# Expert rows added into residual rows in DRAM by an indirect accumulating transfer, tiles loaded back, and the beginning by chunks

## The chip, the cores and the metric

One NeuronCore of a Trainium2 chip runs the whole program. The metric is the device time in microseconds of one execution, the median over several. Engines by their short names in the profile: PE is TensorE, DVE is VectorE, ACT is ScalarE, POOL is GpSimd, SP is SyncE, which here only issues DMAs.

## The reference

A trunk of two layers over 1024 tokens of width 1024, all in float32. Each layer has a mixer (attention in layer 0, a causal convolution module in layer 1) and then a mixture of experts; each is normed and modulated by a conditioning vector and added to x through a gate. Cut to what matters:

```python
for layer in range(DEPTH):                                  # DEPTH = 2
    mod = silu(c) @ w_ada[layer] + b_ada[layer]
    sh1, sc1, g1, sh2, sc2, g2 = split(mod, 6)
    h = rms_norm(x, norm1_g[layer]) * (1 + sc1) + sh1
    y = attention(h) if layer == 0 else conv_module(h)
    x = x + g1 * y
    h = rms_norm(x, norm2_g[layer]) * (1 + sc2) + sh2
    # 16 experts in 4 groups; best group, top 2 in it, weights w normed to sum 1
    for t, (e, w) in routed(h):                             # 2 experts for each token
        moe[t] += w * ((silu(h[t] @ w_gate[e]) * (h[t] @ w_up[e])) @ w_down[e])
    x = x + g2 * moe
return rms_norm(x, final_g)
```

## The kernel before

**Stages.** The program goes through: the modulation's first pieces and the first norm (to 44 us), the projections of attention (to 386), attention (to 740), routing and experts of layer 0 (to 1165), the end of that layer and the convolution module (to 1612), routing and experts of layer 1 (to 2033), the end. x lies in SBUF as eight tiles of 128 tokens (`xtile(t)`), except during attention and where it is read again.

**Units.** The 2048 pairs of token and expert are sorted by expert and cut into units of 32 rows, about 73 in each layer; how many an expert has is known only at run time (`bounds`). A unit's 32 rows are spread as quarters over the 128 partitions, so a row of 1024 is four rows of 256. The token of each slot is in `slot_tok`, made by matmuls of one-hot matrices (L1621). For a unit, GpSimd copies its column of `slot_tok` (L585) and gathers its 128 quarter rows from `h_dram` by an indirect DMA (`gather`, L573), VectorE turns, scales and moves them (L1210, L1212, L1216), TensorE multiplies by gate and up (`gate_up`, L1633), ScalarE takes the silu (L768), VectorE multiplies (L1220) and turns (L1224), TensorE multiplies by down (`down`, L1643), and VectorE multiplies by the gate g2 into one of two buffers `yo` (`keep_y`, L1228). ScalarE's queue then stores the unit's rows with four plain DMAs to `y_dram` (L773). The engines run these in written order, in loops over two units each; TensorE has the order gate_up(b), down(b-1).

**Weights.** SyncE loads 6 MB for each expert into one of three sets as soon as the set is free (L370, L374).

**End of a layer.** When all rows are stored (`rows_stored`), GpSimd gathers for each tile two rows of `y_dram` for each token (L596, 16 DMAs of 512 KB), VectorE adds them, weighted, to x (`combine`, L1276 and L1278), then ScalarE squares for the next norm (L646, L652), VectorE scales (L979), TensorE transposes (L1438), and ScalarE and VectorE keep the halves (`norm_keep`, L659 and L985). After layer 1 the next norm is the final one: L972 writes each row tile to one of two buffers, and SyncE stores it (L462).

**The beginning.** Tiles 0 to 3 are normed and transposed while four pieces of w_ada load, and are kept only once the modulation is made (L1005), since keeping scales and shifts.

Of the kernel before, what the change touches and what calls it, by code (L numbers as in the profile page):

```python
# [37 lines left out]
TABLE = MAXBLK + 4  # L38
PARTS = 4
# [20 lines left out]
def trunk(nc, x, c_col, b_ada, final_g, vec_cols, b_out, b_router, w_router, w_ada, w_qkv, w_o, w_in, w_out,  # L60
# [6 lines left out]
    h_dram = [nc.dram_tensor(f"h_rows{l}", (T, D), f32, kind="Internal").ap() for l in range(2)]  # L67
    y_dram = [nc.dram_tensor(f"expert_rows{l}", (MAXBLK * UNIT, D), f32, kind="Internal").ap() for l in range(2)]

    ctx = ExitStack()  # L70
    with ctx:
# [24 lines left out]
        tokid, tile_first = sb("tokid", [P, TT]), sb("tile_first", [P, TT])  # L96
# [6 lines left out]
        idx_now = sb("idx_now", [P, 2], i32)  # L103
        quarter_of = sb("quarter_of", [P, 1])
# [11 lines left out]
        def hrow(n, t):  # L116
# [48 lines left out]
        ygat = [kv[:, 2 * D * b:2 * D * (b + 1)].rearrange("p (k d) -> p k d", k=2) for b in range(4)]  # L165
        hots = hflat[:, 2304:2304 + TT * (3 * UNIT + TABLE)].bitcast(mybir.dt.bfloat16)
        low_hot, low_row, low_tile = (
            hots[:, 2 * TT * UNIT * k:2 * TT * UNIT * (k + 1)].rearrange("p (n s) -> p n s", s=UNIT) for k in range(3))
        high_hot = hots[:, 6 * TT * UNIT:6 * TT * UNIT + 2 * TT * TABLE].rearrange("p (n b) -> p n b", b=TABLE)
# [16 lines left out]
        ada_loaded = [sem(f"ada_loaded{u}") for u in range(2)]  # L186
        bias_loaded = [sem(f"bias_loaded{u}") for u in range(2)]
# [40 lines left out]
        stored = both("stored")  # L228
        y_gathered = [[sem(f"y_gathered{l}{b}") for b in range(4)] for l in range(2)]
        x_added, rows_stored = both("x_added"), both("rows_stored")  # L230
        y_stored = [[sem(f"y_stored{l}{u}") for u in range(2)] for l in range(2)]
# [97 lines left out]
        def _(sp):  # L329
# [12 lines left out]
            for n in range(FIRST_ADA):  # L342
                sp.dma_start(ada_first[n], w_ada[n]).then_inc(ada_loaded[0] if n == 3 else at_loaded[(n + 2) % 3], 16)
            for j in range(8):
# [17 lines left out]
            for l in range(2):  # L362
                sp.wait_ge(stored[l], 16)
# [45 lines left out]
            for k in range(2):  # L409
                first_expert(0, 0, k)  # L410
# [22 lines left out]
            for j in range(10):  # L433
# [5 lines left out]
                if j == 8:  # L439
                    load_shifted(4)  # L440
# [1441 lines left out]
```

## Time and profile before

| | us |
|---|---|
| runs (3) | 2074.67, 2076.95, 2079.11; median 2076.95 |
| the profiled execution | 2082.66, of which the span 2080.9 |
| PE busy | 1910.5 (92%) |
| DVE, ACT, POOL busy | 1182.0, 487.0, 303.6 |
| mean granted clock | 0.953 |

A row of a timeline gives the start in us, the duration, the engine and line, what it writes and reads, and in brackets how long its engine was idle before and what released it. In the chain of waits, each row is a start, a duration and the work that the end waited for. The DMA share is the mean busy share of the core's 16 DMA engines. Queue q1 is SyncE's, q10 ScalarE's, q0 GpSimd's.

### The profile page before, as it was taken

The numbers are of one execution on the slowest core, as the hardware profiler recorded it, in microseconds if no ns is written. First come the engines' busy times: TensorE is split into PE (matmuls) and PEld (weight loads), VectorE is DVE, ScalarE is ACT, GpSimd is POOL, SyncE is SP. The second block draws the span as 40 slices with busy tenths as digits, with TensorE's granted clock in tenths as the row PEclk, the third lists the DMA queues.
The fourth block names the chain that finished last, engine by engine and source line by source line (L and its number), as shares of the span: only waits on it lengthen the run. The fifth ranks groups of instructions, "written<-read, shape, count | busy, mean of one in ns | idle before, by whom it ended". The sixth has DMA issues, their size and how long they took to land.

```text
span 2080.9 us, 49950 instructions
## 1 busy us (share of the span) xinstructions
PE 1910.5 (92%) x19736; PEld 1184.4 (57%) x19736; DVE 1182.0 (57%) x2105; ACT 487.0 (23%) x1029; POOL 303.6 (15%) x464
## 2 busy tenths in 40 slices
PE   5999999999999968999999589999899699999990
PEld 2444444445666646777777357655444467777770
DVE  3547600378889953333333569999995433333336
ACT  3101000456777730000000230010535000000002
POOL 0001030000000012222222400000001122222223
PEclk8999999899999979999999789999999799999995
DMA  9556620100430098777985803033106899854446
GB/s 393 219 202 258 228 62 0 41 11 11 185 150 1 11 367 301 264 280 289 348 329 210 306 9 107 1 119 109 51 0 240 303 408 407 321 208 172 172 172 257
DMA packets 122491, 391.43 MB, mean 188 GB/s; under 512 B 23808, under 2 KB 44928, under 8 KB 118272
## 3 DMA queue, kind: packets, MB, share of 16 engines
q1 hardware_dynamic: 72432, 303.48, 38.5%
q0 software_dynamic: 21904, 66.99, 9.0%
q10 hardware_dynamic: 28032, 19.17, 3.1%
q8 instruction: 95, 1.56, 0.3%
q14 instruction: 28, 0.23, 0.0%
HBM read 337.33 MB, written 47.49 MB: 185 GB/s over the span
## 4 chain that ended last, share of the span: by engine, by line
PE 84%; DVE 8%; DMA 4%; ACT 1%; issue 1%; SPq 0%; POOL 0%; ACTq 0%; DVEq 0%; POOLq 0%
PE ps L1633 24%; PE ps L1643 12%; PE ps L1685 10%; PE ps L1459 9%; PE ps L1570 5%; PE ps L1514 5%; PE ps L1528 4%; PE ps L1541 4%; PE ps L1553 4%; DVE kv L1343 3%; PE ps L1757 3%; DMA kv<-in_w_ada 2%; PE ps L1722 1%; PE ps L1438 1%; DVE pbuf L1027 1%
## 5 line engine op out<-in xcount | busy, mean ns | idle before, releaser
L1633 PE MATMUL ps<-kv,hT 128*32 128x256 f32 x5504 | 388.4, 380 | 2.1 <-DMA kv<-in_w_gate_up 2.1
L1633 PEld LDWEIGHTS ps<-kv,hT 128*32 128x32 f32 x5504 | 241.3, 110 | 65.4 <-issue 4.3
L1343 DVE SCALAR_TENSOR_TENSOR kv<-kv,cols 128x640 f32<-128x640 f32 (+1 forms) x330 | 266.2, 807 | 11.2
L1685 PE MATMUL ps<-hT,ring 128*128 128x320 f32 (+1 forms) x768 | 225.7, 455 | 6.3 <-ACT hT L659 6.3
L1216 DVE TENSOR_TENSOR hT<-hT,modc 128x256 f32<-128x256 f32 x146 | 62.1, 425 | 296.9 <-PE ps L1633 296.9
L1459 PE MATMUL ps<-hT,ring 128*128 128x512 f32 x512 | 223.8, 598 | 1.6 <-ACT hT L659 1.6
L768 ACT ACTIVATE hT<-ps 128x128 f32<-128x128 f32 x146 | 40.6, 278 | 747.4 <-PE ps L1633 747.4
L1040 DVE TENSOR_TENSOR_SCAN pbuf<-hT 128x128 f32<-128x128 f32 (+7 forms) x128 | 173.3, 1354 | 46.2 <-ACT hT L710 45.8
L1685 PEld LDWEIGHTS ps<-hT,ring 128*128 128x128 f32 x768 | 146.4, 192 | 82.2 <-ACT hT L659 7.0
L1459 PEld LDWEIGHTS ps<-hT,ring 128*128 128x128 f32 x512 | 97.4, 192 | 126.1 <-issue 123.3
L1633 PE MATMUL ps<-ring,hT 128*32 128x256 f32 x2560 | 151.5, 389 | 15.9 <-DVE hT L1216 14.2
L573 POOL DMA_INDIRECT hT<-h_rows,idx_now x150 | 146.2, 974 | 112.6 <-POOL idx_now L585 109.9
L1228 DVE TENSOR_TENSOR hT<-ps,bcC 128x256 f32<-128x256 f32 x146 | 62.0, 425 | 160.4 <-PE ps L1643 159.3
L1633 PE MATMUL ps<-hT 128*32 128x256 f32 x1280 | 146.0, 379 | 0.0
L1633 PEld LDWEIGHTS ps<-ring,hT 128*32 128x32 f32 x2560 | 101.5, 113 | 57.7 <-issue 19.3
L1643 PE MATMUL ps<-kv,hT 128*32 128x256 f32 x2112 | 127.8, 379 | 1.5 <-DVE hT L1224 1.5
L585 POOL COPY idx_now<-slot_tok 128x1 int32 x146 | 48.2, 330 | 455.8 <-DVE hT L1210 455.8
L1633 PEld LDWEIGHTS ps<-hT 128*32 128x32 f32 x1280 | 92.0, 110 | 37.6 <-issue 0.2
L1757 PE MATMUL ps<-ring,hT 128*128 128x512 f32 x256 | 112.4, 593 | 0.0
L1514 PE MATMUL ps<-ring,hT 128*128 128x512 f32 x256 | 110.0, 592 | 0.0
L1027 DVE SCALAR_TENSOR_TENSOR pbuf<-kv,cond,pbuf 128x512 f32<-128x512 f32 x140 | 105.3, 752 | 5.0
L710 ACT ACTIVATE hT<-ps 128x128 f32<-128x128 f32 (+7 forms) x128 | 84.5, 660 | 94.2 <-PE ps L1531 88.4
(251 smaller groups left out, 2395.8 us busy)
## 6 DMA issues: line engine op xcount, KB each, us to landing
kv<-in_w_gate_up SPq DMA_DIRECT2D x136, 512.0 KB
kv<-in_w_ada SPq DMA_DIRECT2D x21, 2048.0 KB, 7.8
ring<-in_w_gate_up SPq DMA_DIRECT2D x80, 512.0 KB
kv<-in_w_down SPq DMA_DIRECT2D x48, 512.0 KB
ring<-in_w_down SPq DMA_DIRECT2D x40, 512.0 KB
hT<-in_w_gate_up SPq DMA_DIRECT2D x40, 512.0 KB
expert_rows<-hT ACTq DMA_DIRECT2D x584, 32.0 KB
ring<-in_w_in SPq DMA_DIRECT2D x32, 512.0 KB, 11.9
```

The costliest lines, as they stand in the source:

```text
L573: pool.indirect_dma_start(out=xg[u], out_offset=None, in_=h_dram[l].rearrange("t (q d) -> (t q) d", q=QUARTERS), in_offset=bass.IndirectOf ...
L710: nc.scalar.activation(omega[:, u, 0:w], z_of(p, u)[:, 0:w], ACT.Sigmoid, scale=-HD ** -0.5).then_inc(omega_done, 1)
L1027: ins = V.scalar_tensor_tensor(ada_sum[k], vslot[u][:, 512 * c:512 * c + 512], cond[:, c:c + 1], ada_sum[k] if c else bias[:, u, :], ALU.m ...
L1040: V.tensor_tensor_scan(pbuf[:, u, D - w:D][:, ::-1], omega[:, u, 0:w][:, ::-1], omega[:, u, 0:w], 1.0, ALU.mult, ALU.bypass).then_inc(scan ...
L1343: ins = V.scalar_tensor_tensor(new, old, w_dw_c[:, c, k:k + 1], new, ALU.mult, ALU.add)
L1459: ins = mm(bank(qk_bank(cc) + half), ring[:, j % 3, 512 * c + P * q:512 * c + P * q + P], hT[:, c, 512 * half:512 * half + 512], start=(c ...
L1514: ins = mm(bank(qk_bank(t) + half), hT[:, c, t * P:(t + 1) * P], ring[:, (4 + half) % 3, 512 * c:512 * c + 512], start=(c == 0), stop=(c = ...
L1570: ins = mm(wo_bank(qb, half), oTs[qb % 2][:, c, :], ring[:, half, 512 * c:512 * c + 512], start=(c == 0), stop=(c == DC - 1))
L1633: ins = mm(bank(0)[UNIT * q:UNIT * (q + 1), 0:2 * P], xT[:, c, :], wset[s][q // 2][:, 512 * c + 256 * (q % 2):512 * c + 256 * (q % 2) + 25 ...
L1643: ins = mm(bank(6)[UNIT * q:UNIT * (q + 1), 0:QUARTER], haT[:, UNIT * f:UNIT * (f + 1)], wdown[s][f][:, QUARTER * q:QUARTER * (q + 1)], st ...
L1685: ins = mm(bank((gates_bank, values_bank)[part](i) + b)[:, 0:w], ring[:, j % 3, 512 * k + P * (c % 4):512 * k + P * (c % 4) + P], hT[:, k, ...
L1757: ins = mm(out_bank(t, half), hT[:, c, t * P:(t + 1) * P], ring[:, (8 + half) % 3, 512 * c:512 * c + 512], start=(c == 0), stop=(c == DC - 1))
```

## The change

Three things. **First**, x goes to DRAM: SyncE stores its eight tiles to `x_dram` before the experts. In each unit, `keep_y` now multiplies by the gate and by the slot's weight, and GpSimd adds the 128 quarter rows into `x_dram` by an indirect accumulating DMA. Empty slots point to 32 rows of padding in front of the tokens. An add waits until the one before it has landed, since both may touch the same row. After the last add SyncE loads the eight tiles back; `combine` and its gathers are gone, and so is the storing of 15 MB of zeros to `y_dram`. **Second**, the slot weights need a table of their own: 64 more matmuls after the 64 of the token table, with one-hot matrices in float32 (they were bfloat16, and the token table took 128). **Third**, in the beginning tiles 0 to 3 are transposed early and copied raw, and then scaled chunk by chunk, each chunk followed by its matmul; the last piece of w_ada comes in halves and the first quarter of w_qkv ahead of the second half of x.

```diff
-            for l in range(2):
-                sp.wait_ge(stored[l], 16)
+            def store_x(l, t):
+                sp.dma_start(x_dram[l][UNIT + t * P:UNIT + (t + 1) * P, :], xtile(t)).then_inc(x_stored[l], 16)
+
+            def load_x_back(l):
+                pairs = sp.value_load(bounds[0:1, E + 1:E + 2], min_val=MINBLK * E // 2, max_val=MAXBLK // 2)
+                for u in range(2):
+                    sp.wait_ge(x_gathered[l][u], 16 * pairs + 16)
+                    sp.wait_ge(y_added[l][u], 16 * pairs)
+                for t in range(TT):
+                    if t >= 4:
+                        sp.wait_ge(x_back[t % 4], 32 * l + 16)
+                    sp.dma_start(xtile(t), x_dram[l][UNIT + t * P:UNIT + (t + 1) * P, :]).then_inc(x_back[t % 4], 16)
...
             experts(1)
-            ends = sp.value_load(bounds[0:1, E:E + 1], min_val=1, max_val=MAXBLK)
-            sp.wait_ge(down_done[1], ends)
+            load_x_back(1)
             sp.dma_start(bcA[:, :], final_g.partition_broadcast(P)).then_inc(g_loaded, 16)
...
+                def add_rows(n, u, before=None):
+                    pool.wait_ge(y_kept[l], n + 2)
+                    nc.gpsimd.tensor_copy(idx_put[:, u:u + 1], slot_tok[:, ds(n, 1)]).then_inc(idx_copied[l], 1)
+                    if before is not None:
+                        pool.wait_ge(y_added[l][1 - u], before)
+                    pool.wait_ge(idx_copied[l], 2 * n + 1)
+                    nc.gpsimd.tensor_copy(w_now[:, u:u + 1], slot_w[:, ds(n + 2, 1)]).then_inc(idx_copied[l], 1)
+                    pool.indirect_dma_start(
+                        out=x_dram[l].rearrange("t (q d) -> (t q) d", q=QUARTERS),
+                        out_offset=bass.IndirectOffsetOnAxis(ap=idx_put[:, u:u + 1], axis=0),
+                        in_=yo[u], in_offset=None, compute_op=ALU.add).then_inc(y_added[l][u], 16)
...
+                with pool.Fori(1, last) as i:
+                    gather_next(2 * i + 2, 0)
+                    add_rows(2 * i, 0, 16 * i)
+                    gather_next(2 * i + 3, 1)
+                    add_rows(2 * i + 1, 1, 16 * i + 16)
...
-                def store(b, half):
-                    act.wait_ge(y_kept[l], b + 2)
-                    for q in range(QUARTERS):
-                        act.dma_start(y_dram[l][ds(b * UNIT, UNIT), QUARTER * q:QUARTER * (q + 1)],
-                                      yo[half][UNIT * q:UNIT * (q + 1), :]
-                                      ).then_inc(y_stored[l][half], 16)
...
-                def keep_y(b, half):
+                def keep_y(b, half, copied=None):
                     dve.wait_ge(down_done[l], b + 1)
-                    V.tensor_tensor(yo[half], bank(6)[:, 0:QUARTER],
-                                    bcC[:, 0:QUARTER], ALU.mult).then_inc(y_kept[l], 1)
+                    if copied is not None:
+                        dve.wait_ge(idx_copied[l], copied)
+                    V.scalar_tensor_tensor(yo[half], bank(6)[:, 0:QUARTER], w_now[:, half:half + 1],
+                                           bcC[:, 0:QUARTER], ALU.mult, ALU.mult).then_inc(y_kept[l], 1)
...
             for t in range(TT + 2):
                 if t < TT:
-                    act.wait_ge(x_added[0], t + 1)
+                    act.wait_ge(x_back[t % 4], 16 * (t // 4 + 1))
                     square(2, t)
                     roots(2, t)
...
-                for k, low in enumerate((low_row, low_tile)):
+                for k, low in enumerate((low_row, low_w)):
                     pe.wait_ge(hot_made[l], k + 1)
                     for n in range(2 * TT):
                         for q in range(QUARTERS):
-                            ins = mm(bank(6)[UNIT * q:UNIT * (q + 1), 0:TABLE], low[:, n, :], high_hot[:, n, :],
-                                     start=(n == 0 and k == 0), stop=(n == 2 * TT - 1 and k == 1),
-                                     skip_group_check=True)
-                ins.then_inc(table_summed[l], 1)
+                            ins = mm(bank(6 - k)[UNIT * q:UNIT * (q + 1), P * k:P * k + TABLE], low[:, n, :],
+                                     high_hot[:, n, :], start=(n == 0), stop=(n == 2 * TT - 1), skip_group_check=True)
+                    ins.then_inc(table_summed[l], 1)
...
-            for t in range(TT // 2):
-                norm_keep(0, t)
+            dve.wait_ge(h_kept, TT // 2)
+            dve.wait_ge(h_kept2, TT // 2)
+            for c in range(DC):
+                first_half = hT[:, c, 0:T // 2]
+                V.tensor_scalar(first_half, first_half, modc[:, 0, 1, c:c + 1], modc[:, 0, 0, c:c + 1], ALU.mult,
+                                ALU.add).then_inc(chunk_made, 1)
```

GpSimd in the loop over the units of layer 0, before; an ISA row holds a wait whose value is in a register:

```order
L585 ISA [waits x_turned0]
L585 COPY idx_now<-slot_tok 128x1
L573 DMA hT<-h_rows,idx_now 128x256 [waits idx_next0,table_made0]
L585 ISA [waits x_turned0]
L585 COPY idx_now<-slot_tok 128x1
L573 DMA hT<-h_rows,idx_now 128x256 [waits idx_next0,table_made0]
```

The same loop after the change, its first unit and the beginning of the second:

```order
L621 ISA [waits x_turned0]
L621 COPY idx_now<-slot_tok 128x1
L607 DMA hT<-h_rows,idx_now 128x256 [waits idx_next0,table_made0]
L627 REGISTER_ALU
L628 ISA [waits y_kept0]
L628 COPY idx_put<-slot_tok 128x1
L630 REGISTER_ALU
L631 ISA [waits y_added01]
L632 ISA [waits idx_copied0]
L632 COPY w_now<-hT 128x1
L633 DMA x_rows<-hT,idx_put 4224x256
L621 ISA [waits x_turned0]
```

Between two gathers there are now two copies and the accumulating DMA, with a wait for the other buffer's accumulating DMA (y_added01 is layer 0, buffer 1) in the queue ahead of the next gather.

SyncE at the end of the program, from the last expert's weights on, before:

```order
L374 DMA kv<-in_w_down 128x1024 [waits down_done1]
L374 DMA kv<-in_w_down 128x1024 x3
L457 TENSOR_LOAD bounds
L457 ISA x2
L459 DMA bcA<-in_final_g 128x1024 [waits down_done1]
L462 DMA out_x<-pbuf 128x1024 [waits final_made] x8
```

And after:

```order
L399 DMA kv<-in_w_down 128x1024 [waits down_done1]
L399 DMA kv<-in_w_down 128x1024 x3
L376 TENSOR_LOAD bounds
L376 ISA x2
L378 ISA
L383 DMA xq<-x_rows 128x1024 [waits x_gathered11,y_added11,y_added10,x_gathered10]
L383 DMA xq<-x_rows 128x1024 x3
L383 DMA xq<-x_rows 128x1024 [waits x_back0]
L383 DMA xq<-x_rows 128x1024 [waits x_back1]
L383 DMA xq<-x_rows 128x1024 [waits x_back2]
L383 DMA xq<-x_rows 128x1024 [waits x_back3]
L494 DMA bcA<-in_final_g 128x1024
```

The load of final_g, which stood alone behind the last down product, stands behind the eight loads of x, and these behind the last gathers and adds.

TensorE in the beginning, from the last modulation piece to the first projection, before:

```order
L1429 MATMUL ps<-ones,kv 128x1 [waits ada_row]
L1429 MATMUL ps<-ones,kv 128x1 x3
L1438 MATMUL ps<-ident,bcA 128x128 [waits h_kept2,h_kept,h_made]
L1438 MATMUL ps<-ident,bcA 128x128 x7
L1438 MATMUL ps<-ident,bcB 128x128 [waits h_kept2,h_kept,h_made]
L1438 MATMUL ps<-ident,bcB 128x128 x7
L1459 MATMUL ps<-hT,ring 128x512 [waits at_loaded0,h_kept2,h_kept]
L1459 MATMUL ps<-hT,ring 128x512 x7
```

And after:

```order
L1474 MATMUL ps<-kv 32x512 [waits last_loaded1]
L1474 MATMUL ps<-kv 32x512 x3
L1482 MATMUL ps<-ones,kv 128x1 [waits ada_row]
L1482 MATMUL ps<-ones,kv 128x1 x3
L1482 MATMUL ps<-ones,kv 128x1 [waits ada_row]
L1482 MATMUL ps<-ones,kv 128x1 x3
L1514 MATMUL ps<-hT,ring 128x512 [waits chunk_made,first_cols_loaded]
L1514 MATMUL ps<-hT,ring 128x512 [waits chunk_made] x7
```

The transposes of tiles 2 and 3 (bcA, bcB) have gone ahead of the last pieces of the modulation, and each matmul of the first projection waits for its own chunk.

## Rows read from the trace of the kernel before

**Rows 1.** Windows: length, busy us of each engine (count), PEclk, DMA share, GB/s.

```profile
786.00:1162.00 376.00, 374.62 (x6880) 270.19 (x6880) 145.50 (x427) 20.03 (x72) 93.56 (x143) 0.99 0.79 292
1641.00:2031.00 390.00, 386.31 (x7077) 279.64 (x7080) 150.21 (x440) 20.59 (x74) 96.31 (x147) 0.99 0.71 266
...
1723.00:1736.00 13.00, 13.00 (x248) 9.49 (x243) 5.60 (x18) 0.56 (x2) 2.61 (x4) 1.00 1.04 408
1905.00:1925.00 20.00, 20.00 (x379) 14.59 (x372) 7.76 (x23) 1.10 (x4) 5.22 (x8) 1.00 0.17 48
```

**Rows 2.** The chain of waits in the expert loop: start, us, what.

```profile
1919.50 1.73 PE ps L1643 x32
1921.22 3.45 PE ps L1633 x64
```

**Rows 3.** Timeline of one unit in layer 1, VectorE and GpSimd.

```profile
1896.02 0.40 DVE L1210 STREAM_TRANSPOSE hT<-hT 128x256 f32<-128x256 f32 x1
...
1896.59 0.33 POOL L585 COPY idx_now<-slot_tok 128x1 int32 x1 [3.13 <-DVE hT L1210]
...
1897.68 0.98 POOL L573 DMA_INDIRECT hT<-h_rows,idx_now  x1 [0.75 <-POOL idx_now L585]
```

**Rows 4.** The chain of waits, first gather of layer 0 and of layer 1.

```profile
779.12 5.75 DMA hT<-h_rows,idx_now
...
1636.52 2.78 DMA hT<-h_rows,idx_now
```

**Rows 5.** Timeline of GpSimd, two gathers' issues.

```profile
1726.73 0.97 POOL L573 DMA_INDIRECT hT<-h_rows,idx_now  x1 [0.75 <-POOL idx_now L585]
...
1913.21 0.97 POOL L573 DMA_INDIRECT hT<-h_rows,idx_now  x1 [0.75 <-POOL idx_now L585]
```

**Rows 6.** GpSimd's queue in 1726.73:1730.6, 1730.6:1732.2, 1914.6:1916: packets, MB, share.

```profile
q0 software_dynamic: 3, 0.01, 0.6%
...
q0 software_dynamic: 48, 0.13, 20.6%
...
q0 software_dynamic: 48, 0.13, 31.8%
```

**Rows 7.** Timeline of VectorE, keep_y of two units, two units apart.

```profile
1983.51 0.42 DVE L1228 TENSOR_TENSOR hT<-ps,bcC 128x256 f32<-128x256 f32 x1 [1.08 <-PE ps L1643]
...
1993.92 0.42 DVE L1228 TENSOR_TENSOR hT<-ps,bcC 128x256 f32<-128x256 f32 x1 [1.14 <-DMA expert_rows<-hT]
```

**Rows 8.** Timeline, end of layer 0.

```profile
1164.73 0.42 DVE L1228 TENSOR_TENSOR hT<-ps,bcC 128x256 f32<-128x256 f32 x1 [2.06 <-PE ps L1643]
...
1178.29 1.06 ACT L646 ACTIVATE oT<-xq 128x1024 f32<-128x1024 f32 x1 [9.57 <-DVE xq L1278]
...
1179.47 0.29 ACT L652 ACTIVATE rstd<-ss,eps 128x1 f32<-128x1 f32 x1
...
1191.27 1.49 ACT L659 ACTIVATE hT<-ps,modc 128x128 f32<-128x128 f32 x4
...
1206.77 11.46 PE L1685 MATMUL ps<-hT,ring 128*128 128x320 f32 x32 [4.73 <-ACT hT L659]
```

**Rows 9.** Timeline, end of the program.

```profile
2032.75 0.33 SPq L459 DMA_DIRECT2D bcA<-in_final_g  x1
...
2076.50 1.28 DVE L972 SCALAR_TENSOR_TENSOR pbuf<-xq,rstd,bcA 128x1024 f32<-128x1024 f32 x1
```

**Rows 10.** DMA issues: count, KB each, median us to landing.

```profile
bcB<-in_x POOLq DMA_DIRECT2D x8, 512.0 KB, 3.6
...
out_x<-pbuf SPq DMA_DIRECT2D x8, 512.0 KB, 4.3
```

**Rows 11.** Groups by shape, 755:790: count, busy us, mean ns, idle before.

```profile
L1621 PE MATMUL ps<-hT 128*32 128x96 bf16 x128 | 2.8, 280 | 8.1 <-issue 8.1
```

**Rows 12.** Timeline, the beginning: first norm_keep of ScalarE, first projection.

```profile
36.97 2.91 ACT L659 ACTIVATE hT<-ps,modc 128x128 f32<-128x128 f32 x8 [19.19 <-DVE modc L1005]
...
43.82 9.22 PE L1459 MATMUL ps<-hT,ring 128*128 128x512 f32 x16 [1.60 <-ACT hT L659]
```

More of the change, by code:

```diff
@@ L66, in trunk @@
     mod_dram = nc.dram_tensor("mod_rows", (2 * 6 * D,), f32, kind="Internal").ap()
[L67 to L68 removed]
+    h_dram = [nc.dram_tensor(f"h_rows{l}", (UNIT + T, D), f32, kind="Internal").ap() for l in range(2)]
+    x_dram = [nc.dram_tensor(f"x_rows{l}", (UNIT + T, D), f32, kind="Internal").ap() for l in range(2)]
     ctx = ExitStack()
@@ L164, in trunk @@
                  [bcA[:, :], bcB[:, :], oT[:, :, :].rearrange("p c t -> p (c t)"), pbuf[:, 0, 0:D]]]
[L165 to L169, printed above, removed]
+        low_hot, low_row, low_w = (spare[:, at * P:at * P + 2 * TT * UNIT].rearrange("p (n s) -> p n s", s=UNIT)
+                                   for at in (1, 24, 28))
+        high_hot = hflat[:, 2304:2304 + 2 * TT * TABLE].rearrange("p (n b) -> p n b", b=TABLE)
+        slot_w = hflat[:, 2304 + 2 * TT * TABLE:2304 + (2 * TT + 1) * TABLE]
         def tmp(n, w=E):
@@ L227, in trunk @@
         down_done, y_kept = both("down_done"), both("y_kept")
[L228 to L231, printed above, removed]
+        weights_made = both("weights_made")
+        zeros_stored, x_stored = sem("zeros_stored"), both("x_stored")
+        x_back = [sem(f"x_back{b}") for b in range(4)]
+        idx_copied = both("idx_copied")
+        y_added = [[sem(f"y_added{l}{u}") for u in range(2)] for l in range(2)]
         dve_step, g_loaded = sem("dve_step"), sem("g_loaded")
@@ L580, in moe @@
                     gather(u)
-                pairs = pool.value_load(bounds[0:1, E + 1:E + 2], min_val=1, max_val=MAXBLK // 2)
-                with pool.Fori(0, pairs) as i:
-                    for u in range(2):
-                        pool.wait_ge(x_turned[l], 2 * i + u + 1)
-                        nc.gpsimd.tensor_copy(idx_now[:, u:u + 1],
-                                              slot_tok[:, ds(2 * i + u + 2, 1)]).then_inc(idx_next[l], 1)
-                        pool.wait_ge(table_made[l], 1)
-                        pool.wait_ge(idx_next[l], 2 * i + u + 1)
-                        gather(u)
@@ L590, in moe @@
[L590 to L599 removed]
+                pool.wait_ge(weights_made[l], 1)
@@ L1243, in moe @@
                     if b == 3:
-                        dve.wait_ge(y_stored[l][0], 16 * QUARTERS)
+                        dve.wait_ge(y_added[l][0], 16)
                     if b:
-                        keep_y(b - 1, (b - 1) % 2)
+                        keep_y(b - 1, (b - 1) % 2, 2 if b == 3 else None)
                     turn_ha(b)
@@ L1288, in _ @@
             moe(0)
-            for t in range(TT + 2):
+            for t in range(TT + 1):
                 if t < TT:
-                    combine(0, t)
-                if 1 <= t <= TT:
-                    norm_scale(2, t - 1)
-                if t >= 2:
-                    norm_keep(2, t - 2)
+                    norm_scale(2, t)
+                if t:
+                    norm_keep(2, t - 1)
             V.memset(u_all[:, :, 0:CW - 1], 0.0)
```

185 lines of the change are left out of this document (115 added, 70 removed).

## The prediction

> **What bounds the kernel now.** I read the windows first, because they give the granted clock and the DMA share of each stage, then the chain of waits, then the timeline of one expert unit, and last the DMA queues in windows of one or two microseconds. The kernel spends 766 of its 2080.9 us in the two expert loops, [rows 1], first two rows. There TensorE is busy without a gap at the granted clock 0.99. In the chain of waits a unit is 3.45 us of L1633 and 1.73 us of L1643, one straight after the other, so a unit takes 5.18 us, [rows 2]. What else runs in the loop is hidden as long as it fits into 5.18 us. [rows 3] is one unit on the other engines. GpSimd copies an index (0.33), waits 0.75 for its own copy, issues the gather (0.98), and then waits for VectorE's next L1210 (the 3.13 in brackets). Two units further on the rows must be there.
>
> The second fact is in the DMA share. Between bursts of weights it is 0.17, within a burst 1.04 at 408 GB/s, [rows 1], last two rows. With these two levels the loop rows say how long the bursts last: (0.79-0.17)/0.87 of 376 us is 268 us, (0.71-0.17)/0.87 of 390 us is 242 us, together 510 us, or 98 of the 146 units.
>
> **The loop after the change.** The expert rows go by an accumulating transfer from GpSimd, not by four plain ones from ScalarE. The order of GpSimd shows the price: in front of each such transfer stands a wait for y_added of the other buffer, which is the transfer of the unit just before. So two of them never overlap, and a unit can't take less than one landing, plus the wake-up, the copy of the weight (0.33) and the gap to the issue. Behind it on GpSimd is queued the gather two units ahead, for which VectorE's L1210 waits, and after that TensorE's next L1633; and VectorE's keep_y waits for the y_added of its own buffer, with the turn of ha and TensorE's L1643 behind it. Before, no store waited for the one before it; VectorE waited only for that two units back.
>
> How long is a landing? No row shows an accumulating one. The nearest rows are the gathers: same queue, 128 rows of 1 KB. [rows 4] have one that landed 2.78 us after its issue began, with weights hardly moving, and one that took 5.75 us in the middle of a burst. The queues agree, [rows 5, 6]: in a burst the gather issued at 1726.73 has 3 packets in the first 3.9 us and its 48 in the 1.6 us after that, landing about 5.3 us after the issue; between bursts the one issued at 1913.21 is done by 1916.0, under 2.8 us. So a small transfer on GpSimd's queue takes about 5.5 us in a burst, and I take that for the accumulating one too. The upper bound is the worst row of a write to DRAM: the stores of the unit whose keep_y stood at 1983.51 held VectorE until 1993.92, [rows 7], which is 9.9 us from their issue. The lower bound is the 2.78.
>
> The period in a burst: 5.5 landing, 0.17 wake-up (as from VectorE's L1210 at 1896.02, ended 1896.42, to the copy at 1896.59), 0.33 copy and an estimated gap of 0.3 (the transfer does not wait for that copy as a gather does with its 0.75), is 6.3 us, so 1.1 more than 5.18. The bursts are a fixed number of bytes, so their 510 us stay; in them now 510/6.3 = 81 units get done, not 98, and 17.5 units are left over: 17.5 x 5.18 = **+91 us**. At the lower bound (2.78+0.8 = 3.6 under 5.18) it is 0; at the upper (10.7) it is 510 x (1-5.18/10.7) = +263 us. Between bursts the period stays 5.18: GpSimd's own time is 2.06 for the gather, [rows 3], and for the add two copies of 0.33, 0.75 and 0.3 between, and 0.98, together 2.7; 4.75 in all, 0.4 under the unit. VectorE's keep_y gets a second factor, one instruction as before; ScalarE loses its four issues and was idle anyway.
>
> The Trainium skill, DMA: Bandwidth & Descriptors, section "Anatomy of one DMA — SWDGE (gpsimd) path", gives a fixed 2.0 us plus bytes/436e3 for such a transfer. For 128 KB that would be an estimated 2.3 us, the period would stay 5.18 and the loop would cost nothing. The gather between bursts agrees (2.78 with its issue); the gather in a burst at 5.75 does not, and by the measurement the rule leaves out what a full set of weight queues does to the landing.
>
> The stores of x in layer 1 (4 MB, some 10 us at 408 GB/s) go out ahead of the loop, between the projection's end and the first unit at 1641. They push the weights of the third expert back by as much; slower units give these the time. I take 0, and up to +10 if the units are not slower.
>
> **The end of layer 0.** Before: last keep_y at 1164.73, then 16 gathers of pairs, two additions per tile; TensorE starts at 1206.77, [rows 8]. After: the last two adds between bursts, each 2.8 to 3 us and 0.8 between, so landed about 6 us after 1165.15; a tile of 512 KB comes 3.6 us after its issue, [rows 10], at 1174.8. Then ScalarE sets the pace: square, its accumulator and root are 1.47 us (1178.29 to 1179.76), norm_keep 1.49, [rows 8]. Seven squares and five norm_keeps stand ahead of the first projection: 7 x 1.47 + 5 x 1.49 = 17.7, with gaps 18.7, so TensorE starts at 1193.5. **-13 us**, between -8 (adds landing as in a burst) and -15.
>
> **The end of the program.** Before: the last output row is made at 2076.50, [rows 9]. After, SyncE issues final_g behind all eight tiles, whereas it stood alone at 2032.75 before, and VectorE's first final row needs it. The tiles are issued from about 2039 (the last units as in layer 0); 4.5 MB at 408 GB/s is 11 us, and the latency is the 3.6 us of one tile, [rows 10], less the 1.3 that its own bytes take at that rate, 2.3; so final_g is there at 2052.5. Then two output buffers set the pace: a store takes 4.3 us, [rows 10], and the row 1.28, so 5.6 us for a pair: rows 0 and 1 by 2055, the last at 2055+17 = 2072, 5 us earlier. **-5 us**; without final_g it would have been -14, and with stores of 6.5 us it is 0.
>
> **The routing table.** The one-hot rows become float32, and 64 matmuls now make the token table, where 128 in bfloat16 did, [rows 11]. Their weight loads are of L1633's kind: 64 take 3.45 us at the full clock, [rows 2], and the clock here is at its lower level, so 6.9 us against about 4.5 from VectorE's low_row on. +2.4 us a layer, **+5** in both; if 96 columns cost 96/256 of 256, it is 0.
>
> **The beginning.** TensorE's first projection stood at 43.82, behind four tiles' norm_keep that could start only with the modulation at 36.97, [rows 12]. Now tiles 0 to 3 are transposed and copied raw before that, and each of eight chunks is scaled by one VectorE instruction (an estimate of at most 0.5 us for 512 columns, half of what ScalarE's square of 1024 takes, [rows 8]) with its matmul behind it: start at about 37.5. The second half of x comes behind 512 KB and not 2 MB of w_qkv, and ScalarE is free to square it at once. So the whole moves by about 6 us: **-6 us**, between 0 (DMA share there 0.95) and -8. The padding of 15 MB that is no longer written ran beside attention, hidden.
>
> **The sum** on the profiled execution's 2082.66: +91 -13 -5 +5 -6 = +72, so 2154.7. The median of the runs is 5.7 us below it: 2149.
>
> **The rivals.**
> A, the accumulating transfer lands within 4.4 us in a burst as well (5.18-0.8). Then all that is left is -13 -5 +5 -6 = -19: 2058, range 2045 to 2070, faster. For it: the packets themselves take 1.6 us, the rest is queueing that this queue might not see when two transfers follow each other. Against: both gathers in bursts that can be dated took over 5 us. Decided by whether y_added comes before or after y_kept. In this rival stands what the Trainium skill's fit (DMA: Bandwidth & Descriptors, the same section) would make of the change.
> B, the landing is that of the late rows, since an add also reads its old rows: midway between 5.5 and the 9.9 of [rows 7], 7.7 us and a period of 8.5: 510 x (1-5.18/8.5) = +199 in place of +91, so 2257. For it: the 9.9 of [rows 7]. Against: only one of 146 stores was that late.
> C, the landing costs a little over 4.4, 4.8 say: period 5.6, +38, 2094. It is inside my range.
> D, gains and loss cancel: needs a period of 5.4 in bursts.
>
> **Chances.** Forecast (2085 to 2205) 0.56, A 0.30, B 0.08, C and D between 2070 and 2085 0.06. Two in ten left out puts the range at 2050 to 2205; the forecast's own is 2085 to 2205. A measurement here tells 0.2% (4 us) from no change: faster by more 0.32, same 0.04, slower 0.64.
>
> **What would show it.** In the loop, L1633 starting every 5.18 us where the DMA share is low and about every 6.3 where it is 1.0; GpSimd's copy of w_now waiting for the DMA of x_rows; TensorE waiting for VectorE's keep_y or ha turn. In the tails, ScalarE without gaps from the first tile on, and VectorE's first final row waiting for final_g. The start of the first projection near 37.5. The forecast is wrong if GpSimd's wait is for y_kept and not for y_added in the bursts; then the unit stays 5.18 and A is right.

## The result and the profile after

The changed kernel takes 2248.22 us (median of 4 runs), the kernel before 2076.80 in the same comparison: ratio 1.0816, 95% interval 1.0801 to 1.0831. The profiled execution has a span of 2248.6 us against 2080.9, so 167.7 us more. Slower was forecast, 2149 us; the time lies 43 us above the upper end of the range.

First the two executions stage by stage. Each number is the distance between two rows of TensorE's timeline, or its end: the first router transpose (L1602 before, L1657 after), the first and last matmul of the expert loop (L1633 and L1643 before, L1687 and L1697 after), the first matmul of the convolution stage (L1685, L1741), and the span.

| stage | before | after | difference | forecast |
|---|---|---|---|---|
| up to the router of layer 0 | 759.8 | 751.2 | -8.6 | -6 |
| routing, layer 0 | 26.7 | 29.7 | +3.0 | +2.4 |
| expert loop, layer 0 (72 units) | 378.2 | 473.3 | +95.1 | |
| end of layer 0 | 42.1 | 34.9 | -7.2 | -13 |
| convolution stage | 410.7 | 411.2 | +0.5 | 0 |
| routing, layer 1 | 23.4 | 31.2 | +7.8 | +2.4 |
| expert loop, layer 1 (74 units) | 391.8 | 474.8 | +83.0 | |
| end | 48.2 | 42.3 | -5.9 | -5 |
| both loops | 770.0 | 948.1 | +178.1 | +91 |

So everything outside the loops sums to -10.4 (forecast -19), and the loops cost twice what was forecast. The windows of the changed kernel: layer 0's loop, layer 1's, a stretch in a burst of weights and one between bursts (columns as in [rows 1]).

```profile
781.00:1254.00 473.00, 403.80 (x6912) 268.92 (x6912) 155.57 (x428) 21.30 (x73) 229.20 (x354) 0.95 0.72 231
1731.50:2206.30 474.80, 413.68 (x7104) 272.88 (x7104) 160.22 (x440) 21.88 (x75) 235.16 (x365) 0.95 0.69 218
1205.00:1236.00 31.00, 24.44 (x424) 15.49 (x415) 7.79 (x22) 1.11 (x4) 10.95 (x17) 0.94 1.04 385
1173.00:1202.00 29.00, 29.00 (x544) 21.07 (x540) 12.34 (x34) 1.48 (x6) 19.95 (x31) 1.00 0.34 55
```

Between bursts TensorE is busy for 29.00 of 29.00 us, as before; in the burst for 24.44 of 31.00. So the loss is in the bursts. Who is waited for stands in the waits of the three engines over the whole run (us in total, times, longest).

```profile
DVE hT L1293 <- DMA x_rows<-hT,idx_put: 373.1, 107, 7.7
...
POOL w_now L632 <- DMA x_rows<-hT,idx_put: 271.6, 96, 5.8
...
DVE hT L1273 <- DMA hT<-h_rows,idx_now: 115.9, 81, 6.5
...
PE ps L1697 <- DVE hT L1287: 86.2, 42, 4.6
PE ps L1687 <- DVE hT L1283: 40.0, 19, 4.9
```

GpSimd's copy of w_now waits for the add of the other buffer, VectorE's keep_y for the add of its own, and behind keep_y stands the turn of ha (L1287) that TensorE's down projection needs. The gathers, which stand behind the adds in GpSimd's queue, come late as well (L1273). That is the queue that the prediction described. Now the size. In the chain of waits (start, us, what) an add takes 3.9 us between bursts, and 7.3 to 8.6 in the burst shown:

```profile
1173.69 3.90 DMA x_rows<-hT,idx_put
...
1202.56 8.56 DMA x_rows<-hT,idx_put
...
1212.05 8.01 DMA x_rows<-hT,idx_put
...
1220.99 7.41 DMA x_rows<-hT,idx_put
...
1229.33 7.27 DMA x_rows<-hT,idx_put
```

Over both loops the chain has 56 adds of more than 5 us: 5.1 to 9.4, median 8.1.

GpSimd's timeline gives the whole period in the burst, from one add's issue to the next, 1212.05 to 1220.99, 8.94 us:

```profile
1212.05 1.60 POOL L633 DMA_INDIRECT x_rows<-hT,idx_put  x1 [0.51 <-issue]
1213.11 0.74 POOL L621 COPY idx_now<-slot_tok 128x1 int32 x1
1214.61 0.99 POOL L607 DMA_INDIRECT hT<-h_rows,idx_now  x1 [0.76 <-POOL idx_now L621]
1215.60 0.20 POOL L628 COPY idx_put<-slot_tok 128x1 int32 x1
1220.29 0.18 POOL L632 COPY w_now<-hT 128x1 f32 x1 [4.49 <-DMA x_rows<-hT,idx_put]
1220.99 1.60 POOL L633 DMA_INDIRECT x_rows<-hT,idx_put  x1 [0.52 <-issue]
```

From 1212.05 to the wake-up at 1220.29 are 8.24 us (landing 8.01 and 0.23 of wake-up), then a copy of 0.18 and 0.52 to the next issue. Of the 144 distances between two adds within a loop, 55 are over 6.5 us, with a mean of 9.03, together 496 us; the other 89 have a mean of 4.91, most of them 4.7 to 4.9 (3.9 landing, 0.9 the rest).

The queues in windows of this add show where 8 us go (packets, MB, share): 1212.05 to 1216.5, then 1216.5 to 1220.2.

```profile
q1 hardware_dynamic: 500, 1.83, 101.1%
...
q1 hardware_dynamic: 305, 1.11, 76.5%
q0 software_dynamic: 190, 0.26, 30.9%
```

For 4.45 us GpSimd's queue has no packet at all, much as with the gather in [rows 6]. (For that gather 3 packets came in the first 3.9 us.) Then 190 packets share the engines with the weights for 3.7 us; the gather of [rows 6] had 48 in 1.6 us. Windows between bursts tell whose they are: 1170.8 to 1172.6 holds one add, 1173 to 1174 one gather.

```profile
q0 software_dynamic: 144, 0.13, 63.9%
...
q0 software_dynamic: 48, 0.13, 45.4%
```

The same 0.13 MB goes in 144 packets for an add and in 48 for a gather. An add and the gather issued behind it have 192, so the 190 are these two, but for 2.

### The profile page after: what moved, and what is told of

It reads as the page before. It is cut to its first block, busy times and chain, and to the rows that moved or that the text cites. A ratio compares the mean times of both kernels' runs of the same rounds, so it can differ in the third digit from the quotient of the medians.

```text
span 2248.6 us, 49894 instructions
## 1 busy us (share of the span) xinstructions
PE 1968.8 (88%) x19992; PEld 1180.6 (53%) x19992; DVE 1165.2 (52%) x2074; ACT 482.3 (21%) x1015; POOL 549.3 (24%) x874
## 4 chain that ended last, share of the span: by engine, by line
PE 46%; DMA 30%; issue 7%; POOL 6%; DVE 6%; ACT 2%; POOLq 1%; SPq 0%; DVEq 0%; ACTq 0%
DMA x_rows<-hT,idx_put 27%; PE ps L1741 10%; PE ps L1514 8%; PE ps L1625 5%; PE ps L1569 5%; PE ps L1583 3%; PE ps L1596 3%; PE ps L1608 3%; DVE kv L1399 3%; PE ps L1813 3%; POOL hT L607 2%; POOL x_rows L633 2%; POOL idx_now L621 1%; PE ps L1687 1%; POOL w_now L632 1%
## 5 line engine op out<-in xcount | busy, mean ns | idle before, releaser
L1687 PE MATMUL ps<-kv,hT 128*32 128x256 f32 x5504 | 401.3, 388 | 12.2 <-DVE hT L1283 11.7
L1293 DVE SCALAR_TENSOR_TENSOR hT<-ps,w_now,bcC 128x256 f32<-128x256 f32 x146 | 70.6, 484 | 423.8 <-DMA x_rows<-hT,idx_put 373.1
L1687 PEld LDWEIGHTS ps<-kv,hT 128*32 128x32 f32 x5504 | 240.6, 113 | 87.1 <-DVE hT L1279 18.5
L633 POOL DMA_INDIRECT x_rows<-hT,idx_put x146 | 234.3, 1605 | 80.4 <-issue 75.9
L1741 PE MATMUL ps<-hT,ring 128*128 128x320 f32 (+1 forms) x768 | 226.2, 456 | 6.0 <-ACT hT L711 6.0
L1741 PEld LDWEIGHTS ps<-hT,ring 128*128 128x128 f32 x768 | 146.6, 192 | 81.9 <-ACT hT L711 6.5
L1687 PE MATMUL ps<-ring,hT 128*32 128x256 f32 x2560 | 155.6, 397 | 26.2 <-DVE hT L1283 13.6
L1687 PE MATMUL ps<-hT 128*32 128x256 f32 x1280 | 154.7, 396 | 14.7 <-DVE hT L1283 14.7
L1697 PE MATMUL ps<-kv,hT 128*32 128x256 f32 x2112 | 134.4, 395 | 25.6 <-DVE hT L1287 25.5
L1687 PEld LDWEIGHTS ps<-ring,hT 128*32 128x32 f32 x2560 | 99.3, 115 | 78.8 <-issue 23.1
L1273 DVE STREAM_TRANSPOSE hT<-hT 128x256 f32<-128x256 f32 x146 | 63.9, 438 | 119.1 <-DMA hT<-h_rows,idx_now 115.9
L1687 PEld LDWEIGHTS ps<-hT 128*32 128x32 f32 x1280 | 91.4, 115 | 65.0 <-DVE hT L1279 19.0
L1697 PEld LDWEIGHTS ps<-kv,hT 128*32 128x32 f32 x2112 | 81.6, 113 | 66.2 <-issue 29.9
L621 POOL COPY idx_now<-slot_tok 128x1 int32 (+1 forms) x146 | 110.8, 759 | 15.4 <-DVE hT L1273 15.4
L1697 PE MATMUL ps<-ring,hT 128*32 128x256 f32 x1280 | 85.9, 411 | 30.4 <-DVE hT L1287 30.4
L1813 PE MATMUL ps<-ring,hT 128*128 128x512 f32 x256 | 112.4, 593 | 0.0
## 6 DMA issues: line engine op xcount, KB each, us to landing
ring<-in_w_qkv SPq DMA_DIRECT2D x5, 2048.0 KB, 12.3
```

The lines of the kernel that those rows point to most:

```text
L621: nc.gpsimd.tensor_copy(idx_now[:, u:u + 1], slot_tok[:, ds(n + 2, 1)]).then_inc(idx_next[l], 1)
L633: pool.indirect_dma_start(out=x_dram[l].rearrange("t (q d) -> (t q) d", q=QUARTERS), out_offset=bass.IndirectOffsetOnAxis(ap=idx_put[:, u: ...
L1687: ins = mm(bank(0)[UNIT * q:UNIT * (q + 1), 0:2 * P], xT[:, c, :], wset[s][q // 2][:, 512 * c + 256 * (q % 2):512 * c + 256 * (q % 2) + 25 ...
L1697: ins = mm(bank(6)[UNIT * q:UNIT * (q + 1), 0:QUARTER], haT[:, UNIT * f:UNIT * (f + 1)], wdown[s][f][:, QUARTER * q:QUARTER * (q + 1)], st ...
L1741: ins = mm(bank((gates_bank, values_bank)[part](i) + b)[:, 0:w], ring[:, j % 3, 512 * k + P * (c % 4):512 * k + P * (c % 4) + P], hT[:, k, ...
L1813: ins = mm(out_bank(t, half), hT[:, c, t * P:(t + 1) * P], ring[:, (8 + half) % 3, 512 * c:512 * c + 512], start=(c == 0), stop=(c == DC - 1))
```

## The experiments

Theory T: in this kernel an accumulating transfer waits for the one before it, one takes about 8.2 us while weights are loaded, and that sets the time of a unit. Rival G: it is GpSimd's own work; its accumulating issue takes 1.60 us, the gather 1.00. Rival B: the reads and writes of the adds take the weights' bandwidth and lengthen the bursts. (This is not the prediction's B.)

**Two targets, nothing waits for the add before.** Leaves the rows of odd units out of the output. Adds into one target still keep their order, since VectorE refills a buffer only after that buffer's add has landed.

```
-                    if before is not None:
-                        pool.wait_ge(y_added[l][1 - u], before)
...
-                        out=x_dram[l].rearrange("t (q d) -> (t q) d", q=QUARTERS),
+                        out=(x_dram, odd_dram)[u][l].rearrange("t (q d) -> (t q) d", q=QUARTERS),
```

> The rows of odd units go by the same accumulating transfer into a second, zeroed tensor in DRAM that nothing reads, so their share is missing from the output (layer 1 may then choose a few other experts), and no transfer waits for the one before it; GpSimd issues the same instructions. Theory T (two accumulating transfers may not overlap, and in a burst of weights one takes about 8.2 us): the loop of layer 0 falls from 473 us to 378 to 390, the whole from 2248 to 2072 (2062 to 2088). Rival G (GpSimd's own work, 1.60 us for the accumulating issue beside 1.00 for the gather and the waits between, fills the unit): the loop stays above 460, the whole above 2230. Rival B (the read and the write of each add take the weights' bandwidth, and the bursts last longer): the loop stays above 440, since the same bytes move.

Measured: 2069.4 us, ratio 0.9953 (0.9935 to 0.9971). Loops 379.6 and 394.6 us, 774.2 together, with the same number of matmuls:

```profile
781.00:1160.60 379.60, 375.80 (x6912) 271.43 (x6912) 152.41 (x428) 21.36 (x73) 238.65 (x356) 1.00 0.87 288
1633.70:2028.30 394.60, 387.98 (x7104) 275.27 (x7104) 155.46 (x440) 21.92 (x75) 244.76 (x366) 0.99 0.80 262
```

GpSimd is busy for 238.65 us, more than the 229.20 with the wait, and moves the same bytes (288 GB/s for 379.6 us is 109 MB, as is 231 GB/s for 473.0); 173.9 of the 178.1 us are gone. G and B fall. The edit takes away the wait and changes the target, so one has to see whether the adds themselves became quick. They did not. In a burst of this run (GpSimd's timeline; its queue in 1019.2:1022.6, while 1017.3:1019.2 has no packet of it; a row of the chain):

```profile
1014.46 1.60 POOL L636 DMA_INDIRECT x_rows<-hT,idx_put  x1 [0.52 <-DVE hT L1276]
...
1019.71 1.60 POOL L636 DMA_INDIRECT odd_rows<-hT,idx_put  x1 [0.51 <-issue]
...
q0 software_dynamic: 192, 0.26, 33.8%
...
1154.84 7.20 DMA odd_rows<-hT,idx_put
```

The 192 packets are, by their count, the add issued at 1014.46 and the gather behind it. They move only about when the next add is issued, 5.25 us later, and an add that the chain dates took 7.20 us. So T holds: it is the wait between the adds, not the adds. The end of layer 0 is 29.8 us here and the end of the program 38.5, against 34.9 and 42.3, so the late last adds had also cost 5.1 and 3.8 us there.

**Plain rows, same waits.** The transfer overwrites; the sum is missing from the output.

```
-                        in_=yo[u], in_offset=None, compute_op=ALU.add).then_inc(y_added[l][u], 16)
+                        in_=yo[u], in_offset=None).then_inc(y_added[l][u], 16)
```

> The same indirect transfer without the addition, so it overwrites the rows and the output lacks the sum (layer 1 may choose other experts); all waits stay. T, with the term of the prediction right for a plain transfer and wrong for an adding one: a transfer lands in 2.8 to 3 us between bursts and in 5.5 to 6 in one, the period in a burst falls from 9.0 to about 6.4, the loop of layer 0 takes 400 to 430 us in place of 473, the whole 2120 to 2170. If the addition costs nothing and every indirect write to DRAM is that slow: landing still 8.2 in a burst, loop 465 to 480, the whole 2235 to 2255. G: no change, since GpSimd does the same.

Measured: 2161.61 us, ratio 1.0394 (1.0374 to 1.0414); loop of layer 0 416.7 us (layer 1 chose other experts and has 78 units, so only layer 0 compares). Both numbers lie in the forecast of T, the landing and the period (about 7.4 us, mean of those over 6.5) not quite. The chain has

```profile
800.18 6.18 DMA x_rows<-hT,idx_put
807.30 6.10 DMA x_rows<-hT,idx_put
...
842.68 7.21 DMA hT<-h_rows,idx_now
...
1012.89 6.84 DMA x_rows<-hT,idx_put
1020.67 6.35 DMA x_rows<-hT,idx_put
...
1886.60 5.41 DMA hT<-h_rows,idx_now
```

and over both loops 56 plain writes of more than 5 us: 5.2 to 8.3, median 6.2, where the adds had 8.1. So the addition costs about 1.9 us of landing in a burst. Its issue alone is 0.6 longer: 1.60 us with the addition, here

```profile
L633 POOL DMA_INDIRECT x_rows<-hT,idx_put x150: 983/1014/1247, 794.6 to 2124.6; - x150
```

(minimum, median, maximum in ns). A plain write has 48 packets like a gather (a window from 1200.5 to 1202.0 between bursts of this run holds them). So of the 2.6 us that the prediction's landing lacked (5.5 for 8.1), about 1.9 belong to the addition, with its longer issue and three times the packets; which of these two weighs more isn't separated. The other 0.7 is no cost of a write in place of a read as far as this run shows: its gathers under weights took 5.4 to 7.2 us too (two are shown), so 5.5 was near the low end for a gather as well.

**Light weights in layer 1.** Experts 3 to 14 of layer 1 load 256 of each 1024 columns.

```
+                cols = {"cols": 256} if l else {}
...
-                        load_down(s, w_down[ds(3 * i + s + l * E, 1)].rearrange("a p n -> (a p) n"))
+                        load_down(s, w_down[ds(3 * i + s + l * E, 1)].rearrange("a p n -> (a p) n"), **cols)
```

> In layer 1 the weights of experts 3 to 14 are loaded to a quarter only (256 of each 1024 columns), the rest of the tile stays as it was, so the output is not the reference's; the choice of experts and the number of units stay. T with the bursts as the cause of the long landing: adds of layer 1 land in 3.9 us except in short bursts, the loop of layer 1 takes 388 to 405 us in place of 475, the whole 2160 to 2182. G: the loop stays at 475, the whole at 2248. If the landing were long for another reason than the weights (rows far apart in DRAM, a read before each write), the loop would stay above 460.

(load_gate_up takes the same argument.) Measured: 2167.38 us, ratio 1.0425 (1.0403 to 1.0448). Layer 1's loop takes 393.6 us, layer 0's, unchanged, 473.9:

```profile
780.00:1254.00 474.00, 405.41 (x6912) 266.38 (x6912) 156.27 (x428) 21.24 (x73) 228.50 (x354) 0.94 0.72 231
1730.00:2123.60 393.60, 386.93 (x7104) 278.06 (x7104) 154.58 (x440) 21.81 (x75) 239.91 (x364) 0.99 0.51 119
```

All waits and instructions are there, only the weights' bytes are gone, and with them 81.2 of the 83.0 us. Of layer 1's 73 distances between adds only 4 are over 6.5 us, where there were 26. So the long landing comes from the traffic of weights, and not from the rows' places in DRAM or from the order of instructions.

**2 MB of weights at a time.** SyncE waits for the first 2 MB of an expert's gate and up weights to land before it issues the second 2 MB. The wait stands in the loop over both halves, so SyncE also waits for the second 2 MB before the down weights, which the expectation leaves out.

```
                             load_gate_up(s, k, w_gate_up[ds(6 * i + 2 * s + 2 * l * E + k, 1)].rearrange("a p n -> (a p) n"))
+                            sp.wait_ge(w_loaded[s][k], 16 * PARTS * i + 16 * PARTS * (l * (5, 6, 5)[s] + 1))
```

> The changed kernel, but SyncE issues the second 2 MB of an expert's gate and up weights only when the first 2 MB have landed, so that at most four 512 KB transfers are outstanding where there were eight. If an add lands late whenever the weights move at full rate, however much is queued behind them: the bursts hold the same bytes, loops within 10 us of 948 together, the whole 2240 to 2256. If the late landing comes from the depth of the backlog: landing in a burst falls from 8.2 towards 5, the whole 2130 to 2200.

Measured: 2329.65 us, ratio 1.1199 (1.1171 to 1.1226), outside both forecasts. Loops 520.2 and 510.1 us. VectorE's wait for the adds grew from 373.1 us to

```profile
DVE hT L1294 <- DMA x_rows<-hT,idx_put: 484.2, 103, 8.7
```

In layer 0, 38 of the 71 distances between adds are over 6.5 us (29 of 71 before this edit), and these still take 7.7 to 10.9 us, 9.20 in the mean; the adds of more than 5 us in the chain have a median of 8.1, as before it. So the landing does not shrink with the backlog; with shorter bursts and gaps between them, more adds touch a burst, and one that touches a burst pays nearly in full. That last step is read from the counts and not shown by a run of its own. My first forecast, that only the bytes of a burst count, is wrong: their division counts too.

**The beginning alone** (on the kernel before): raw tiles kept, chunks scaled, w_qkv in columns.

```
...
+            for c in range(DC):
+                first_half = hT[:, c, 0:T // 2]
+                V.tensor_scalar(first_half, first_half, modc[:, 0, 1, c:c + 1], modc[:, 0, 0, c:c + 1], ALU.mult,
+                                ALU.add).then_inc(chunk_made, 1)
...
```

> The kernel before with the beginning of the changed one alone (raw tiles kept, chunks scaled by one instruction each, w_qkv in columns, the last piece of w_ada and the first of w_qkv in parts). The trace of the changed kernel has attention 8 us earlier, so 2068.5 us (2066 to 2071), ratio 0.996. The rival: the 8 us are there but something later waits for a transfer that starts no earlier, ratio 0.998 to 1.001.

Measured: 2071.43 us, ratio 0.9963 (0.9950 to 0.9976), 0.4 us above the range that was expected. The router of layer 0 starts at 751.8 (759.8 before), and each stage behind it keeps its length within 2 us. This part is a small gain by itself, 0.4%, and this kernel, whose output is complete, is faster than both the one before and the changed one.

**Narrow stores of x in layer 1.** 128 of 1024 columns are stored; the output lacks most of x.

```
-                sp.dma_start(x_dram[l][UNIT + t * P:UNIT + (t + 1) * P, :], xtile(t)).then_inc(x_stored[l], 16)
+                w = P if l else D
+                sp.dma_start(x_dram[l][UNIT + t * P:UNIT + (t + 1) * P, 0:w], xtile(t)[:, 0:w]).then_inc(x_stored[l], 16)
```

> In layer 1 only the first 128 of 1024 columns of x are stored ahead of the loop (the rest of the tensor is zero), so the output lacks most of x; 3.5 MB less are moved there. The stretch from the last router product to the first expert in layer 1 takes 31.2 us in the changed kernel, 29.7 in layer 0 without such stores, 23.4 before. If the stores cause the difference to layer 0 and push the weights back: 4 to 8 us less there, the whole 2241 to 2245. If the float32 table alone does it: no change, 2246 to 2250.

Measured: 2241.15 us, ratio 1.0778 (1.0757 to 1.0799). Routing in layer 1 is 26.5 us in place of 31.2 and the loop 470.3 in place of 474.8. Routing before was 23.4, and 26.5 is the +3.0 of the float32 table that layer 0 shows as well. So the stores cost 4.7 us ahead of the loop, and perhaps as much again in it (one profile).

**final_g first.** It is issued behind the last projection, ahead of the wait for the adds.

```
+            ends = sp.value_load(bounds[0:1, E:E + 1], min_val=1, max_val=MAXBLK)
+            sp.wait_ge(down_done[1], ends)
+            sp.dma_start(bcA[:, :], final_g.partition_broadcast(P)).then_inc(g_loaded, 16)
             load_x_back(1)
-            sp.dma_start(bcA[:, :], final_g.partition_broadcast(P)).then_inc(g_loaded, 16)
```

> The changed kernel with final_g issued as soon as the last projection is done, ahead of the wait for the adds and of the eight tiles. In its trace VectorE's first final row starts at 2230.1 behind final_g, and tile 0's root was ready at 2220.7; from then on two output buffers set the pace. So the end moves by up to 9 us: 2239 us (2237 to 2243). If the tiles' own landing or ScalarE's squares set the end, 2245 to 2249.

Measured: 2242.92 us, ratio 1.0780 (1.0756 to 1.0803), and an end of 39.1 us for 42.3: 3 us, not 9. The whole lies at the edge of the expected range, with luck: in this profile the router of layer 0 also starts 2.3 us earlier, which the edit doesn't touch. The first row now starts early, but SyncE issues the first store only behind the eight tiles, the store lands 7.1 us after its issue, and the third row waits for it (timeline of VectorE, and SyncE's tiles and stores):

```profile
2211.73 7.83 SPq L383 DMA_DIRECT2D xq<-x_rows  x8
...
2216.71 1.28 DVE L1021 SCALAR_TENSOR_TENSOR pbuf<-xq,rstd,bcA 128x1024 f32<-128x1024 f32 x1
...
2219.61 18.80 SPq L499 DMA_DIRECT2D out_x<-pbuf  x8
2226.72 1.28 DVE L1021 SCALAR_TENSOR_TENSOR pbuf<-xq,rstd,bcA 128x1024 f32<-128x1024 f32 x1 [7.24 <-DMA out_x<-pbuf]
```

That the store was slow because the tiles' bytes stood ahead of it is read from this order; no run shows it by itself.

**Two targets, both loaded back and summed**, the complete form of the first experiment.

```
+                    sp.dma_start(odd_tile[t % 4], odd_dram[l][rows, :]).then_inc(x_back[t % 4], 16)
...
+                V.tensor_tensor(xtile(t), xtile(t), odd_tile[t % 4], ALU.add).then_inc(x_whole, 1)
...
```

> Odd units add into a second, zeroed tensor, no transfer waits for the one before it, both tensors are loaded back tile by tile and summed by one VectorE instruction each; final_g first. The output is complete. From the run with two targets (2069.4, no second load): -9 for final_g, +10 to +15 for 4 MB more to load in each tail and eight additions of about 1.1 us on VectorE: 2073 us (2064 to 2080), ratio to before 0.993 to 1.000. If the second load costs nothing, 2060; if the tails go at the pace of 8 MB at 408 GB/s with latency in front, 2085.

Measured: 2087.36 us, ratio 1.0036 (1.0020 to 1.0052), 7 us above the range that was expected. The loops stay repaired (379.3 and 397.9), but the second load costs 7.0 us in the end of layer 0 (36.8 for 29.8) and 8.4 in the end of the program (46.9 for 38.5), though final_g went first. There VectorE's third row stands for 10.22 us:

```profile
2054.36 1.29 DVE L1028 SCALAR_TENSOR_TENSOR pbuf<-xq,rstd,bcA 128x1024 f32<-128x1024 f32 x1
...
2056.92 1.29 DVE L1028 SCALAR_TENSOR_TENSOR pbuf<-xq,rstd,bcA 128x1024 f32<-128x1024 f32 x1
...
2060.23 22.82 SPq L504 DMA_DIRECT2D out_x<-pbuf  x8
...
2069.66 1.28 DVE L1028 SCALAR_TENSOR_TENSOR pbuf<-xq,rstd,bcA 128x1024 f32<-128x1024 f32 x1 [10.22 <-DMA out_x<-pbuf]
```

SyncE issues the store of the first output row at 2060.23, 4.6 us after that row was made (2054.36 and 1.29), since its list has all sixteen loads first; 9.4 us after that issue the third row is free to go. The forecast had also counted 9 us for final_g, and the run above gave 3. So the complete form takes 10 us more than the kernel before: it repairs the change, but isn't a gain. Stores on another queue weren't tried.

## Why the prediction was wrong, step by step

**The mechanism was right, one term was mis-sized.** The prediction took 5.5 us for the landing of an accumulating transfer in a burst, from the gather of [rows 4, 6]. It is 8.1 in the median, 8.0 in the add shown. That step failed: "same queue, 128 rows of 1 KB" makes a gather and an accumulating write alike, and they are not. The plain rows (median 6.2) and the adding ones (8.1, with 144 packets for 48) show that most of the difference comes with the addition. The bounds of 2.78 to 9.9 held it, and the rival with 7.7 us and a period of 8.5 had almost its size, but got a chance of 0.08; its 2257 lies 9 us from the measured time. Its reason, that an add also reads its old rows, is a guess that no run here tests. With an unknown operation that reads and writes, the value should have lain nearer to the late write of [rows 7] than to a read.

**The period** was taken as the landing and 0.8 us; measured 0.93 (0.23, 0.18, 0.52). 6.3 was forecast for a burst, and it is 9.03.

**The length of the bursts** was forecast at 510 us; the long periods sum to 496. The way to this number is right. By it 510 x (1-5.18/9.03) = +217 would come out, and +178 was measured. Counted instead from the periods: 55 x (9.03-5.18) = +212, less 89 x (5.18-4.91) = 24, is +188. These 24 us the prediction left out: between bursts an add follows the last after 4.91 us and not 5.18, so GpSimd catches up with the lag that the burst left, while TensorE goes on at 5.18. Of the 10 us that remain, 7 lie behind the loops: the last adds are issued at 1261.76 and 2211.51, 7.6 and 5.2 us after their loops' ends, where the run with two targets has 3.5 and 2.1.

**A slip** in rival C: a landing of 4.8 gives +38 on A's 2058, which is 2096 and not 2094. Nothing rests on it.

**The rule of the Trainium skill** (DMA: Bandwidth & Descriptors, "Anatomy of one DMA — SWDGE (gpsimd) path") would have made it an estimated 2.3 us and no loss. Even between bursts the add takes 3.9, in one 8.0; the measurement decides, and the light weights show that the traffic of weights makes the difference between the last two.

**End of layer 0:** -13 forecast, -7.2 measured. The last adds had landed not 6 us after the last projection but 11.3 (the tiles are issued at 1265.50, the loop ended at 1254.2), because the adds lagged behind TensorE. The first tile came 6.4 us after its issue and not 3.6, a value taken from another queue's transfers in [rows 10]; from there to the first projection ScalarE took 17.1 us, where 18.7 was forecast.

```profile
1265.50 10.58 SPq L383 DMA_DIRECT2D xq<-x_rows  x8
...
1271.95 1.06 ACT L698 ACTIVATE oT<-xq 128x1024 f32<-128x1024 f32 x1 [10.44 <-DMA xq<-x_rows]
```

Without the lag, in the run with two targets, the end of layer 0 is 12.3 us shorter than before, close to the forecast.

**The end:** -5 forecast, -5.9 measured, and that is partly luck. The first final row waits for final_g, as said, but 23.8 us after the last projection and not 19.8, mostly since the last adds were late here too (the tiles are issued 9.2 us after it, where 6.3 was forecast):

```profile
2230.10 0.17 DVE L1015 RECIPROCAL rstd<-rstd 128x1 f32<-128x1 f32 x1 [23.18 <-DMA bcA<-in_final_g]
...
2243.82 1.28 DVE L1019 SCALAR_TENSOR_TENSOR pbuf<-xq,rstd,bcA 128x1024 f32<-128x1024 f32 x1
```

From there to the last row it took 13.7 us, where 19.5 was forecast: with the tiles all loaded an output store lands in 2.6 us (median), not in the 4.3 of [rows 10], so a pair of rows takes 4.0 us and not 5.6. The two errors nearly cancel. Nor would the end have been 14 us shorter without the wait for final_g: the run with final_g first, late adds included, ends 9.1 us shorter than before.

**The table:** +2.4 a layer forecast, +3.0 measured. **The stores of x in layer 1:** the prediction took 0 and up to +10; 4.7 us were visible in the routing, where no slow unit can hide them. By which transfer they delay the first unit isn't shown.

**The beginning:** start of the first projection forecast at 37.5, and -6; measured 35.34, and -8.6, a little beyond its bound of -8. A chunk takes 0.47 us (eight in 3.74), as taken. What the prediction left out is that the modulation itself came 2.3 us earlier (34.65 for 36.97 in [rows 12]). Only 0.6 of it is an earlier start of its last piece. The other 1.7 is the clock: before, TensorE had stood idle for 2.00 us and ran this piece at a granted clock of 0.53, close to its lower level (1.2 of 2.4 GHz); now the early transposes fill that place, it works without a gap from 20.00 on, and the same 16 matmuls run at 1.00 (before, then after).

```profile
30.97 3.61 PE L1421 MATMUL ps<-kv 128*32 128x512 f32 x16 [2.00 <-DMA kv<-in_w_ada]
...
30.34 1.92 PE L1474 MATMUL ps<-kv 128*32 128x512 f32 x16
...
34.65 3.74 DVE L1067 TENSOR_SCALAR hT<-hT,modc 128x512 f32<-128x512 f32 x8
...
35.34 8.80 PE L1514 MATMUL ps<-hT,ring 128*128 128x512 f32 x16 [1.20 <-DVE hT L1067]
```

## What to carry to other kernels

When each read-modify-write transfer waits for the one before it, they form a chain with one landing per link. A link costs the landing and about 0.9 us here, and whatever of it exceeds the time of a unit is lost: nothing at 4.8 us, nearly 4 us a unit at 9.0. Look first for a transfer that waits for another transfer, and ask how long one takes while the weights move, not alone. A second target took the wait away and gave back 174 of 178 us, but reading it back cost 15 us in the two tails, and the complete form ended 10 us slower than the kernel before; so price the way back too. GpSimd gave 24 us of its lag back between bursts, since it is a little faster than TensorE there.

## What the runs showed of the hardware

Transfers of 128 rows of 1 KB issued from GpSimd, between bursts and while weights move at 385 to 408 GB/s: gather 2.78 and 5.3 to 5.75 us in the kernel before, 5.4 to 7.2 in bursts of the run with plain rows; plain scattered write 6.2 in a burst (median of 56); accumulating write 3.9 and 8.1 (median of 56). In a burst the add shown has no packet for 4.45 us after its issue, and the gather of [rows 6] 3 packets in 3.9 us. The issue of an accumulating one holds GpSimd for 1.60 us, of a plain one for 1.01. The 0.13 MB of an accumulating one take 144 packets, those of a plain write or a gather 48. With at most 2 MB of gate and up weights outstanding for 4 MB, an add in a burst takes 8.1 us as before.

With the waits for the adds, the granted clock of layer 0's loop is 0.95, and its matmuls are busy for 403.8 us where the same 6912 took 375.8 in the run with two targets at 1.00. These 28 us seem to lie inside the waits, since the adds set the pace; no run separates them.
